# High weight part first: a float32-accurate block on one core, with the order of its products changed and two rows of the experts' third matrices to a partition

## What is computed

```python
for e in range(N_EXPERTS):                                   # 32
    a = jax.nn.silu(hf @ w_e_gate[e]) * (hf @ w_e_up[e])     # [256,1024] @ [1024,512], twice
    out = out + gates[:, e:e+1] * (a @ w_e_down[e])          # [256,512] @ [512,1024]
```

## Time and profile before

| | |
|---|---|
| median of three runs | 1810.47 us (1810.31 to 1811.44) |
| the profiled execution | 1807.79 us |
| its span | 1805.9 us |
| PE busy | 1685.9 us (93%), 11478 matmuls |
| DVE busy | 1288.3 us (71%) |
| ACT busy | 1022.0 us (57%) |
| DMA | 393.96 MB, mean 218 GB/s |
| granted clock, mean | 0.979 |

### The profile page before, as it was taken

The page is one execution under the profiler, slowest core; times in us unless marked ns, Lnnn a source line. Parts: engine busy times, 40 slices in busy tenths (PEclk is TensorE's granted clock), DMA queues, the critical chain, the costliest instruction groups (busy, mean ns, idle before and its releaser), DMA issues.

```text
span 1805.9 us, 29847 instructions
## 1 busy us (share of the span) xinstructions
PE 1685.9 (93%) x11478; PEld 1506.0 (83%) x11478; DVE 1288.3 (71%) x1439; ACT 1022.0 (57%) x1127; POOL 63.8 (4%) x56
## 2 busy tenths in 40 slices
PE   8999989889999999999998879799999999799998
PEld 7998868868877666666668868799999999699997
DVE  6545687665589999999997876575556878575554
ACT  4333465454578988888987454353334484343432
POOL 0000000000000000000006400000000020000000
PEclk9999999889999999999999989999999999899999
DMA  9562114065699999999998324246554455245540
GB/s 324 183 186 77 41 59 156 8 258 202 229 359 419 419 419 420 420 420 408 415 395 288 123 96 140 91 144 211 182 186 146 159 188 186 70 156 195 181 145 24
DMA packets 195503, 393.96 MB, mean 218 GB/s; under 512 B 6960, under 2 KB 152112, under 8 KB 179024
## 3 DMA queue, kind: packets, MB, share of 16 engines
q1 hardware_dynamic: 193744, 386.11, 59.1%
q0 software_dynamic: 1664, 6.52, 1.0%
HBM read 379.77 MB, written 12.85 MB: 217 GB/s over the span
## 4 chain that ended last, share of the span: by engine, by line
PE 75%; DVE 11%; issue 5%; ACT 5%; DMA 4%; SPq 0%; DVEq 0%; ACTq 0%; POOLq 0%
PE ps L652 14%; PE ps L653 13%; PE ps L654 13%; DVE wlo L1852 4%; ACT whi L1279 3%; PE ps L966 3%; PE ps L968 3%; PE ps L967 3%; PE ps L778 3%; PE ps L897 2%; PE ps L898 2%; PE ps L934 2%; PE ps L802 2%; PE ps L888 2%; PE ps L889 2%
## 5 line engine op out<-in xcount | busy, mean ns | idle before, releaser
L1852 DVE TENSOR_TENSOR wlo<-raw,whi 128x2048 fp32r<-128x2048 f32 (+3 forms) x358 | 813.4, 2281 | 249.1 <-ACT whi L1279 244.6
L1279 ACT ACTIVATE whi<-raw 128x2048 fp32r<-128x2048 f32 (+3 forms) x358 | 673.3, 1889 | 357.4 <-PE ps L654 253.1
L652 PE MATMUL ps<-xh,whi 128*128 128x256 f32 x936 | 272.1, 291 | 14.7 <-DVE xl L1865 9.9
L653 PE MATMUL ps<-xl,whi 128*128 128x256 f32 x936 | 267.8, 286 | 0.0
L654 PE MATMUL ps<-xh,wlo 128*128 128x256 f32 x936 | 267.5, 286 | 0.0
L652 PE MATMUL ps<-xb_h,whi 128*128 128x256 f32 x768 | 218.8, 285 | 5.2 <-DVE arena L1934 5.2
L654 PE MATMUL ps<-xb_h,wlo 128*128 128x256 f32 x768 | 218.3, 284 | 0.0
L653 PE MATMUL ps<-xb_l,whi 128*128 128x256 f32 x768 | 218.2, 284 | 0.0
L652 PEld LDWEIGHTS ps<-xh,whi 128*128 128x128 f32 x936 | 182.4, 195 | 20.1 <-issue 18.3
L653 PEld LDWEIGHTS ps<-xl,whi 128*128 128x128 f32 x936 | 182.7, 195 | 0.2
L654 PEld LDWEIGHTS ps<-xh,wlo 128*128 128x128 f32 x936 | 182.6, 195 | 0.0
(11 more groups left out here) (409 smaller groups left out, 2944.1 us busy)
## 6 DMA issues: line engine op xcount, KB each, us to landing
raw<-w_e_gate_dram SPq DMA_DIRECT2D x64, 1024.0 KB, 8.3
raw<-w_e_up_dram SPq DMA_DIRECT2D x64, 1024.0 KB, 8.7
raw<-w_e_down_dram SPq DMA_DIRECT2D x64, 1024.0 KB, 8.2
raw<-ffn_w_gate_up_dram SPq DMA_DIRECT2D x44, 1024.0 KB, 5.1
raw<-w_in_dram SPq DMA_DIRECT2D x30, 1024.0 KB, 5.6
raw<-ffn_w_down_dram SPq DMA_DIRECT2D x22, 1024.0 KB, 4.9
raw<-xa_w_kv_dram SPq DMA_DIRECT2D x16, 1024.0 KB, 5.9
raw<-xa_w_q_dram SPq DMA_DIRECT2D x8, 1024.0 KB, 5.1
```

Source lines behind the costliest of these rows:

```text
L652: mm = nc.tensor.matmul(o, wh, h, start=first and a == 0, stop=False, skip_group_check=not group)
L653: nc.tensor.matmul(o, wh, l, start=False, stop=False, skip_group_check=not group)
L1279: nc.scalar.activation(whi[u % HL][:, 0:n], raw[u % RAW][:, 0:n], ACT.Copy).then_inc(hi_ready, 1)
L1852: v.tensor_tensor(wlo[u % HL][:, 0:n], raw[u % RAW][:, 0:n], whi[u % HL][:, 0:n].bitcast(F32), ALU.subtract).then_inc(lo_ready, 1)
```

## The change

1. `wdn` is read with two neighbouring rows on each partition, one run of 8 KB. The contraction index that a partition holds is changed by that, so `turn_hidden` takes every second column of the hidden rows (`features`).
2. In `feature_unit` (whole units), `token_unit`, `gu`, both `down` and the experts' `unit`, all products with `whi` come first, after a wait for `hi_ready` alone, and then all with `wlo`, after a wait for `lo_ready`. `triple` with both waits stays in the halves of units between attention steps, in the opening unit of a norm and some small ones.
3. In a light tile, `down` waits only for `hid_h` before its first matmul, and for `hid_l` ahead of the last four of the first half.

The number of matmuls and their shapes are the same. The diff, cut to its core:

```diff
-            wdn = t["w_e_down"][0].rearrange("e (h k p) n -> h e p k n", p=P, h=2)
+            wdn = t["w_e_down"][0].rearrange("e (h p k) n -> h e p k n", p=P, h=2)
...
+            def high_first(o, blocks, u, i=None):
+                fresh, st["fresh"] = st["fresh"], False
+                high_in(u, i)
+                for b, parts in enumerate(blocks):
+                    for a, (wh, wl, h, l) in enumerate(parts):
+                        if fresh and b == 0 and a % 2 == 0:
+                            split_in()
+                        nc.tensor.matmul(o[b], wh, h, start=b == 0 and a == 0, stop=False, skip_group_check=True)
+                        nc.tensor.matmul(o[b], wh, l, start=False, stop=False, skip_group_check=True)
+                low_in(u, i)
+                for b, parts in enumerate(blocks):
+                    for a, (wh, wl, h, l) in enumerate(parts):
+                        mm = nc.tensor.matmul(o[b], wl, h, start=False,
+                                              stop=b == len(blocks) - 1 and a == len(parts) - 1,
+                                              skip_group_check=True)
+                return mm
...
 def token_unit(u, part=None, parts=1):
-                steps = [(tt, k) for tt in range(2) for k in range(kc)]
+                both = [(tt, k) for tt in range(2) for k in range(kc)]
+                steps = [(p, tt, k) for p in range(2) for tt, k in both]
                 if part is not None:
                     steps = steps[part * len(steps) // parts:(part + 1) * len(steps) // parts]
...
 def unit(u, m, up, part, i=None):
-                    weights_in(u, i, 6 * LOOP)
+                    high_in(u, i, 6 * LOOP)
...
+                        for k in range(4):
+                            nc.tensor.matmul(o, h[:, k, :], wh[:, k, :], start=part == 0 and k == 0, stop=False)
+                            if m < HEAVY:
+                                nc.tensor.matmul(o, l[:, k, :], wh[:, k, :], start=False, stop=False)
+                    low_in(u, i, 6 * LOOP)
+                    for s in passes(m):
+                        for k in range(4):
+                            mm = nc.tensor.matmul(ps[:, s % 2 + 2 * up, :], rows[s][0][:, k, :], wl[:, k, :], start=False,
+                                                  stop=part == 1 and k == 3)
                         if m < TWICE and up and part and s % 2 == 0:
                             mm.then_inc(first_done, 1)
...
+                def features(src, k):
+                    return src.rearrange("s (h p k) -> s h k p", h=2, k=2)[:, k // 2, k % 2, :]
...
-                                                      src[first % 2][:, k * P:k * P + P], both, start=True, stop=True)
+                                                      features(src[first % 2], k), both, start=True, stop=True)
...
 def down(half, u, m, i=None):
+                    high_in(u, i, 6 * LOOP)
                     if half == 0:
-                        pe.wait_ge(r_hid_l, add + last + 1)
+                        pe.wait_ge(r_hid_l if m < HEAVY else r_hid_h, add + last + 1)
                         if first >= 1:
                             pe.wait_ge(r_y, add + first)
...
+                    rows_by(hid_h, wh, start=half == 0)
+                    if half == 1:
+                        rows_by(hid_l, wh)
+                        low_in(u, i, 6 * LOOP)
+                        rows_by(hid_h, wl, stop=True).then_inc(unit_used, 1)
+                    else:
+                        low_in(u, i, 6 * LOOP)
+                        rows_by(hid_h, wl)
+                        pe.wait_ge(r_hid_l, add + last + 1)
+                        rows_by(hid_l, wh).then_inc(unit_used, 1)
```

More of the change, by code:

```diff
@@ L669, in feature_unit @@
                 if half != 1:
-                    weights_in(u)
                     if bank is None:
@@ L846, in down @@
                     for c in range(DC):
-                        mm = triple(ps[:, c // 2, (c % 2) * T:(c % 2 + 1) * T],
-                                    [(wh[:, k, c * P:c * P + P], wl[:, k, c * P:c * P + P],
-                                      ah[:, 2 * (j % 2) + k, :], al[:, 2 * (j % 2) + k, :]) for k in range(2)],
-                                    first=first and c % 2 == 0, last=last, group=False)
+                        o, cols = ps[:, c // 2, (c % 2) * T:(c % 2 + 1) * T], slice(c * P, c * P + P)
+                        for k in range(2):
+                            nc.tensor.matmul(o, wh[:, k, cols], ah[:, 2 * (j % 2) + k, :],
+                                             start=first and c % 2 == 0 and k == 0, stop=False, skip_group_check=True)
+                            nc.tensor.matmul(o, wh[:, k, cols], al[:, 2 * (j % 2) + k, :], start=False, stop=False,
+                                             skip_group_check=True)
+                    low_in(u, i)
+                    for c in range(DC):
+                        o, cols = ps[:, c // 2, (c % 2) * T:(c % 2 + 1) * T], slice(c * P, c * P + P)
+                        for k in range(2):
+                            mm = nc.tensor.matmul(o, wl[:, k, cols], ah[:, 2 * (j % 2) + k, :], start=False,
+                                                  stop=last and k == 1, skip_group_check=True)
                         if last and c in (1, 3, 5):
@@ L882, in gather @@
                     mm.then_inc(gath_mm, 1)
[L884 to L899 removed]
                 def unit(u, m, up, part, i=None):
                     add = 0 if i is None else i * LOOP
[L904 removed]
+                    high_in(u, i, 6 * LOOP)
                     wh, wl = wview(whi, u, 4, 512), wview(wlo, u, 4, 512)
+                    four = slice(4 * part, 4 * part + 4)
+                    rows = {}
                     for s in passes(m):
                         if m == 0:
[L908 removed]
+                            rows[s] = xc_h[:, :, s * P:s * P + P][:, four, :], xc_l[:, :, s * P:s * P + P][:, four, :]
                         else:
[L910 removed]
+                            rows[s] = got_h[s % 2][:, four, :], got_l[s % 2][:, four, :]
                         if m and not up and not part:
@@ L915, in unit @@
                                 pe.wait_ge(r_silu, s - 1)
-                        four = slice(4 * part, 4 * part + 4)
-                        bank = s % 2 + 2 * up
-                        if m < HEAVY:
-                            mm = product(bank, wh, wl, h[:, four, :], l[:, four, :], part == 0, part == 1)
-                        else:
-                            mm = product_pair(bank, wh, wl, h[:, four, :], part == 0, part == 1)
+                        h, l = rows[s]
+                        o = ps[:, s % 2 + 2 * up, :]
+                        for k in range(4):
[7 more added lines that the diff above has]
+                                                  stop=part == 1 and k == 3)
                         if m < TWICE and up and part and s % 2 == 0:
@@ L952, in down, with rows_by @@
                     first, last = passes(m)[0], passes(m)[-1]
-                    weights_in(u, i, 6 * LOOP)
+                    wh, wl = wview(whi, u, 2, D), wview(wlo, u, 2, D)
+                    w = P if m < HEAVY else SLOTS
+                    def rows_by(src, weights, start=False, stop=False):
+                        for s in passes(m):
+                            for n in range(2):
+                                o, cols = ps[0:w, 4 + 2 * (s - first) + n, :], slice(512 * n, 512 * n + 512)
+                                for k in range(2):
+                                    mm = nc.tensor.matmul(o, src[s % 2][:, 2 * half + k, 0:w], weights[:, k, cols],
+                                                          start=start and k == 0, stop=stop and k == 1)
+                        return mm
@@ L954, in down @@
+                    high_in(u, i, 6 * LOOP)
                     if half == 0:
-                        pe.wait_ge(r_hid_l, add + last + 1)
+                        pe.wait_ge(r_hid_l if m < HEAVY else r_hid_h, add + last + 1)
                         if first >= 1:
                             pe.wait_ge(r_y, add + first)
-                    wh, wl = wview(whi, u, 2, D), wview(wlo, u, 2, D)
-                    w = P if m < HEAVY else SLOTS
-                    for s in passes(m):
-                        for n in range(2):
-                            o, cols = ps[0:w, 4 + 2 * (s - first) + n, :], slice(512 * n, 512 * n + 512)
-                            for k in range(2):
-                                h = hid_h[s % 2][:, 2 * half + k, 0:w]
-                                l = hid_l[s % 2][:, 2 * half + k, 0:w]
-                                nc.tensor.matmul(o, h, wh[:, k, cols], start=half == 0 and k == 0, stop=False)
-                                nc.tensor.matmul(o, h, wl[:, k, cols], start=False, stop=False)
-                                mm = nc.tensor.matmul(o, l, wh[:, k, cols], start=False, stop=half == 1 and k == 1)
```

76 lines of the change are left out of this document (37 added, 39 removed).

## The result

The changed kernel takes 1798.9 us, median of six runs (1796.5 to 1801.2), the kernel before, run beside it, 1810.2 us (1804.4 to 1811.4). The ratio is 0.9948, 95% interval 0.9935 to 0.9961: 9.4 us less by the ratio, 11.3 by the two medians. The profiled execution took 1798.25 us with a span of 1796.4 us, for 1807.79 and 1805.9. Measured once more at the end beside another kernel, the ratio was 0.9945 (0.9929 to 0.9960).

A forecast was written before the change was run, and what follows sets the result against it. PE was taken to set the light tiles' pace by a hair, the DMAs 0.3 us behind. Terms 3.7 + 1.2 + 2.1 + 2.0 + 1.4 - 1.4 = 9.0 us gave 1798.8 profiled, 1801.5 us median; range 1794 to 1808.

The forecast's parts named there:

- The experts' first unit: Start of the experts' stage: PE starts without waiting for `wlo`, 2.2 us, and keeps the fast clock, 1.5 us; 3.7 in all.
- Where the DMAs fill up: From 517 to 536 us: DMA time left unused because loads come late is won back, 1.2 us, between 0 and 1.9.
- Light tiles: Experts' light tiles: the `hid_l` wait goes, loads set the pace, a tile falls from 15.9 to 15.6 us; gain 2.1 us.
- rows of 8 KB: Third-matrix loads, 536 to 932 us: larger packets save 0.08 us a tile, 2.0 us in 25 tiles, between 0 and 16.
- PE's 1.44 us a tile: Light tiles: PE waits 28.8 us in 20 tiles for `hid_l`, so PE alone would need 14.5 us a tile.
- rival C: Turn of each light tile: the step of two columns is dear, total 1814 us, near 1850 at 192 ns a load; chance 0.07.
- Turning with a step of two: Turn of the hidden rows in light tiles: costs nothing to 3.1 us a tile, taken as 0 since PE has 1.1 to spare.
- Memory units: Units of the last layer's memory: PE starts with `whi` and no longer waits while `wlo` is made, gain 1.4 us.
- Fresh units: Four units whose low activations come in pieces: PE waits for the pieces, a loss of 0.35 us each, 1.4 in all.
- The feed-forwards have no waits for weights: Feed-forward layers: no wait for weights to remove, so no gain or loss was put into the sum.
- A (larger packets give much more): Third-matrix loads: the 8 KB rows give 16 us in place of 2.0, total 1787.5 us; chance 0.09.
- B (the loads hide all): Experts' stage: DMAs lose time for their own reasons, 8 KB rows give nothing, only 3.7 us remain, total 1806.8 us; chance 0.20.

The follow-up runs named there:

- rows alone: The kernel before with only the 8 KB rows and the turn that reads every second column, old order of products: 1809.4 us, ratio 1.0010.
- less bytes: The changed kernel with half of each third matrix left unread in 20 light tiles, all products still made: 1780.3 us, measured once.
- order alone: The changed kernel with third matrices in the old 4 KB rows and the turn reading neighbouring columns: 1802.1 us, ratio 0.9974.
- experts-alone kernel: The changed kernel with the change in the experts' stage only, all units outside it in the old order: 1797.1 us, ratio 0.9945.
- both mirrored kernels: The two kernels rows alone and order alone, with ratios 1.0010 and 0.9974 to the kernel before.

## Why the prediction was right, and where it was not

The total was right, 9.0 us forecast and 9.4 measured, and the main mechanism was. That the two agree to 0.4 us is luck. In the trace of the changed kernel the forecast terms come to 10.4 us (3.8 + 1.3 + 3.7 + 1.9 - 0.3), a loss that I missed takes 3.2 of them, and some 2 us are the lead with which that execution reached the experts (-2.37), which no term has.

*The experts' first unit, 3.7 us.* Right in place and size: 3.8 us in the table and 3.7 to 3.8 in all traces with the early start, 4.0 by the kernel that puts the wait back. The clock stayed at full speed, as I had assumed. PE began at 374.66, not at 377.1; the 2.4 us between are the lead with which this execution reached the stage (-2.37 in the table).

*Where the DMAs fill up, 1.2 us.* 1.3 us in the table, 406 GB/s for 380. But the second run of the same kernel loses 0.2 us there, and rows alone win 0.8 without the new order, so the term by itself is not shown. Together with the next one it is: from DVE's 505.5 us to the landing of the last third matrix the changed kernel wins 5.6 us and its second run 5.5, for 1.2 + 4.1.

*Light tiles and rows of 8 KB, 2.1 + 2.0 us.* Right in mechanism and size. The loads take over as the limit (less bytes: 14.8 us a tile), and without the shorter wait nothing is won. A tile takes 15.50 us, as predicted. PE and DVE win 0.43 us in each tile, 8.2 us by the end of the stage, but "nor is 0.3 x 20 the gain" holds: the landing time fell by 4.0 us over the stage before and now stays, and that part is only lead used up. Counted where the limit is, the loads win 4.3 us from 568.9 us to the last landing (order alone 1.5, so the rows add 2.8), and the sums are gathered 3.7 us further ahead, for 4.1. "What the loads win arrives there in full; the stores and the gather behind it keep their lengths" holds within 1.4 us of the gather.

*PE's 1.44 us a tile.* A misreading. The 28.8 us of the earlier trace rows are in the row of the weight loads (PEld), which start their wait ahead of the products. PE's own row of the same view has less:

```profile
PE ps L966 <- DVE al L2110: 20.4, 20, 1.1
```

That is 1.02 us a tile, so PE alone needed 14.9 us, not 14.5; less bytes shows 14.8. PE had 0.7 us to spare for the turn, not 1.1, and rival C decided from some 45 ns a load, not 88. Nothing in the sum hangs on it, since the loads need 15.5.

*Rows of 8 KB alone.* 0.08 us a tile predicted, 0.10 measured; that is 2.3 us inside the stage by DVE, 2.8 by the landings, and 2.9 us by the end of the trace, for 2.0. The ratios say 4.7 us, with intervals wide enough for 3. The far end, 16 us, is out. The Trainium skill (DMA: Bandwidth & Descriptors, Why small descriptors are slow) led to an estimate of 0.06 us a tile; the measured 0.10 is nearer to it than to the 0.64 of two matrices alone.

*Turning with a step of two, 0.* It is 0.09 us a tile, 1.82 for 1.73. The Trainium skill (SBUF — State Buffer, Door 1: The DMA port swizzle) counts a step of up to four float32 as free; the trace shows nearly that, 6 ns a weight load. Behind the loads it costs nothing.

*Memory units, 1.4 us.* 1.9 in the table, and in all traces with the new order there: PE no longer waits there at all.

*Fresh units, -1.4 us.* Mis-sized: 0.3 us at one of the four. The 0.9 us by which their waits seem to have grown have nothing to do with the order: the sum is 9.9 us in the kernel with the new order alone and in the experts-alone kernel, and 10.7 in the kernel with the rows alone, which has the old order; it is the longest of the four waits that is 3.2 or 4.0 us.

*What was missed.* "The feed-forwards have no waits for weights" is true, and I stopped there. I had followed `first_done`, the signal that moves back inside a unit of the experts, and not `sums_there`, which does the same in the last unit of a feed-forward layer, where no cover is behind it. 2.9 to 3.8 us at the first of the two layers and 0.3 at the second.

Of the rivals, A (larger packets give much more) is refuted by both mirrored kernels, C (a dear step) by the 1.82 us. B (the loads hide all) is refuted by the rates: 413 GB/s from 784 to 912 us before, 420 with the order alone, 423 with the rows as well. It named rightly that the loads set the end, which is why 8 KB rows matter at all.

## What to carry to other kernels

When products are put in order of which operand comes first, look for every signal that leaves the middle of the unit: the last pass then holds back all its sums, and the reader at the end of a layer has nothing else to do; there the old order is better (here 3.2 and 4.1 us by two pairs of traces, 4 to 5 by ratios and medians). Where two engines are within 3% of each other, a gain for the one lasts only until the other's lead is used up. So count a gain at the engine that limits, here by when each load lands: counted at DVE it was 8.2 us, of which 4.3 were there at the end. And lay the start times of the same instructions of two kernels side by side: it finds gains and losses that cancel, which the total hides.

## What the runs showed of the hardware

- Behind the first feed-forward layer one wait of 1.48 us left PE's clock at 1.00 in all seven traces with the old order there. With the new order PE waited three times and the clock fell to 0.50 in all seven: in three after waits of 1.30 and 1.41 or 1.42 us, in four one wait later. It cost up to 0.9 us over the 2.88 that the later sums cost.
- The same kernel differed by 1.3 us between two executions by when the clock first rose (first table, 118.9 us), and medians of the kernel before ranged from 1807.8 to 1811.0 us between calls. A step that several traces share is better evidence for 2 us than the medians are.
- The share of DMA time was 1.01 to 1.02 whether PE or the loads set the pace, and 0.98 with 5 MB a tile for 6. The time from issue to landing told them apart: 11.1 falling to 7.1 us with PE at the limit, 11.0 staying with the loads.
- With all loads in 4 KB packets or up, 420 GB/s (order alone) turned into 423 (changed) when the third matrices went to 8 KB, at a share of DMA time that fell from 1.02 to 1.01.
